# First tokens ahead of the conditioning weights in the load queue, and the opening of TensorE's list rewritten to the order of arrival

## The reference, cut to what matters

```python
shift, scale, gate = jnp.split(mod, 3, axis=-1)          # mod = silu(c) @ w_ada + b_ada
h = rmsnorm(x, rms_g) * (1 + scale) + shift
q, k, v, z_a, glu, z_b, gates = jnp.split(h @ w_in + b_in, PROJ_SPLITS, axis=-1)
```

## Time and profile before

| what | value |
|---|---|
| median of 3 runs | 1874.22 us (1873.65 to 1875.42) |
| the profiled execution, its own time | 1877.82 us |
| its span in the trace | 1875.6 us |
| TensorE busy in the span | 1829.8 us, 98% |
| chain of work that ended last, share of TensorE | 90% |

### The profile page before, as it was taken

How to read it: one execution, slowest core, us unless ns; L and a number is a source line. 1 busy time by engine, 2 the same in 40 slices (tenths; PEclk the granted TensorE clock), 3 DMA queues, 4 the chain that set the end, 5 groups by cost and what they waited for, 6 DMA issues and landing times.

```text
span 1875.6 us, 27263 instructions
## 1 busy us (share of the span) xinstructions
PE 1829.8 (98%) x10723; PEld 1561.1 (83%) x10723; DVE 1015.1 (54%) x1710; ACT 542.0 (29%) x1061; POOL 122.8 (7%) x205
## 2 busy tenths in 40 slices
PE   6999999999999999999999999999999899999998
PEld 3788899988888888888888888888888888888886
DVE  3544512111098338816870996766768555654444
ACT  3731101021111111211110114667768222322221
POOL 0100000000000000000000004322330000000000
PEclk9999999999999999999999999999999999999999
DMA  9524423143022112211220164997887767653321
GB/s 318 169 89 158 144 68 132 49 140 115 12 78 89 65 34 82 76 40 59 72 80 20 65 153 119 211 178 163 175 182 176 229 205 244 193 191 140 141 101 56
DMA packets 211145, 235.08 MB, mean 125 GB/s; under 512 B 47707, under 2 KB 157131, under 8 KB 207819
## 3 DMA queue, kind: packets, MB, share of 16 engines
q1 hardware_dynamic: 210760, 233.24, 42.5%
q10 hardware_dynamic: 259, 0.11, 0.0%
HBM read 152.52 MB, written 80.78 MB: 124 GB/s over the span
## 4 chain that ended last, share of the span: by engine, by line
PE 90%; SPq 4%; DMA 2%; issue 1%; ACT 1%; DVE 1%; POOLq 0%; DVEq 0%; POOL 0%; ACTq 0%
PE banks L789 17%; PE banks L790 17%; PE banks L791 17%; PE banks L1742 4%; PE banks L1741 4%; PE banks L1743 4%; PE banks L1713 3%; PE banks L1715 3%; PE banks L1714 3%; PE banks L1225 3%; SPq L1093 2%; PE banks L784 2%; PE banks L785 2%; PE banks L786 2%; PE banks L1191 2%
## 5 line engine op out<-in xcount | busy, mean ns | idle before, releaser
L789 PE MATMUL banks<-h_hi,w_hi 128*128 128x512 f32 (+1 forms) x1600 | 593.3, 371 | 3.6 <-DVE h_lo L598 2.5
L790 PE MATMUL banks<-h_lo,w_hi 128*128 128x512 f32 (+1 forms) x1600 | 589.4, 368 | 0.0
L791 PE MATMUL banks<-h_hi,w_lo 128*128 128x512 f32 (+1 forms) x1600 | 589.3, 368 | 0.0
L730 DVE SCALAR_TENSOR_TENSOR conv_acc<-glu_out,taps,conv_acc 128x773 f32<-128x773 f32 x360 | 371.5, 1032 | 12.3
L789 PEld LDWEIGHTS banks<-h_hi,w_hi 128*128 128x128 f32 x1600 | 301.8, 189 | 57.6 <-issue 3.4
L791 PEld LDWEIGHTS banks<-h_hi,w_lo 128*128 128x128 f32 x1600 | 301.8, 189 | 50.7
L790 PEld LDWEIGHTS banks<-h_lo,w_hi 128*128 128x128 f32 x1600 | 302.0, 189 | 49.0
L506 ACT ACTIVATE out_stage<-banks,param_cols 128x512 f32<-128x512 f32 (+1 forms) x120 | 77.0, 647 | 439.2 <-PE banks L791 433.2
L1713 PE MATMUL banks<-y_hi,wp_hi 128*128 128x512 f32 (+1 forms) x320 | 120.0, 375 | 4.9 <-DVE m_sum L1935 2.8
L1332 ACT ACTIVATE probs<-scores,stat 128x640 f32<-128x640 f32 (+2 forms) x128 | 106.7, 834 | 60.2 <-DVE stat L1259 58.6
L1715 PE MATMUL banks<-y_hi,wp_lo 128*128 128x512 f32 (+1 forms) x320 | 118.4, 370 | 0.0
(11 more groups left out here) (161 smaller groups left out, 2397.5 us busy)
## 6 DMA issues: line engine op xcount, KB each, us to landing
proj<-out_stage SPq DMA_DIRECT2D x96, 256.0 KB, 2.0
w_raw<-in_w_in SPq DMA_DIRECT2D x44, 512.0 KB, 3.9
gates_in<-proj SPq DMA_DIRECT2D x64, 256.0 KB, 2.9
k_hi<-k_hi_rows SPq DMA_DIRECT2D x16, 640.0 KB, 13.2
k_lo<-k_lo_rows SPq DMA_DIRECT2D x16, 640.0 KB, 15.2
w_ada<-in_w_ada SPq DMA_DIRECT2D x8, 1024.0 KB, 10.8
x_out<-in_x_sample SPq DMA_DIRECT2D x16, 512.0 KB, 3.4
out_y_sample<-x_out SPq DMA_DIRECT2D x15, 512.0 KB, 2.6
```

Source lines behind the costliest of these rows:

```text
L730: op = dve.scalar_tensor_tensor(dst, src, tap, dst, ALU.mult, ALU.add)
L789: pe.matmul(out, w_hi[:, s, k], h_hi[c][:, k], start=first, stop=False)
L790: pe.matmul(out, w_hi[:, s, k], h_lo[c][:, k], start=False, stop=False)
L791: op = pe.matmul(out, w_lo[:, s, k], h_hi[c][:, k], start=False, stop=last)
```

## The change

The change reorders the lists of the opening; no product is added or removed.

- SyncE: chunk 0's tokens are loaded first, in two halves with a semaphore each, and then the quarters of the conditioning weights, each followed by one column block. Before, quarter 0 came first, then the tokens.
- GpSimd: `RMS` has seven entries instead of six, since chunk 0 is done in halves.
- ScalarE and VectorE: the squares and the normalization of chunk 0 stand before the first row copy and the first coefficients; `modulate`, `split`, `high` and `low` stand in pairs behind the quarter that they need. On VectorE the two halves of chunk 1's normalization stand before and after `split(7)`.
- TensorE: `turn(0)` to `turn(2)` stand ahead of `ada_products(0)`; `ada_products(1)` stands ahead of the first `step`; the products of the three units are grouped by quarter, and `turn(8)` stands ahead of `step(6, [0, 1])`.
- The semaphore of the v bias serves chunk 0's first half as well, and is waited for at 32 where the bias is needed.

```diff
-RMS = [(0, 0, 4), (1, 0, 2), (1, 2, 2), (2, 0, 4), (4, 0, 2), (3, 0, 4)]
+RMS = [(0, 0, 2), (0, 2, 2), (1, 0, 2), (1, 2, 2), (2, 0, 4), (4, 0, 2), (3, 0, 4)]
...
-            if c == 1:
-                sp.dma_start(xs[c][:, 0:2], src[:, 0:2]).then_inc(x_half_in, 16)
+            if c < 2:
+                sp.dma_start(xs[c][:, 0:2], src[:, 0:2]).then_inc(x_half_in[c], 16)
                 sp.dma_start(xs[c][:, 2:4], src[:, 2:4]).then_inc(x_in[c], 16)
...
+        load_x(0)
         load_ada(0)
-        load_x(0)
+        load_w(sp, 0)
         load_ada(1)
-        load_w(sp, 0)
+        load_w(sp, 1)
         load_ada(2)
-        load_w(sp, 1)
+        load_w(sp, 2)
         load_ada(3)
-        load_w(sp, 2)
         load_x(1)
...
+        squares(0, 0)
+        squares(0, 1)
         row_of(0)
-        squares(0)
         high(0)
+        modulate(0)
+        modulate(1)
         row_of(1)
-        for s in range(4):
-            modulate(s)
         high(1)
+        modulate(2)
+        modulate(3)
+        high(2)
         row_of(2)
         modulate(4)
         modulate(5)
         row_of(3)
-        high(2)
         squares(1, 0)
...
+        normalize(0)
+        normalize(1)
         coefficients(0)
-        normalize(0)
         low(0)
+        split(0)
+        split(1)
+        low(1)
         coefficients(1)
-        for s in range(4):
-            split(s)
-        low(1)
+        split(2)
+        split(3)
+        low(2)
         coefficients(2)
         split(4)
         split(5)
-        low(2)
         coefficients(3)
         split(6)
+        normalize(2)
         split(7)
-        normalize(1)
-        normalize(2)
+        normalize(3)
...
-        ada_products(0)
         pe.wait_ge(rows_in, 16 * 7)
         pe.transpose(ps_rows, rows[0:R_C, :], cst.ident[0:R_C, 0:R_C]).then_inc(turned, 1)
         pe.transpose(ps_taps, taps[0:4 * TAPS, :], cst.ident[0:4 * TAPS, 0:4 * TAPS]).then_inc(turned, 1)
-        turn_row(0)
         pe.wait_ge(cols_out, 2)
-        ada_products(1)
         for s in range(3):
             turn(s)
+        ada_products(0)
+        turn_row(0)
+        ada_products(1)
+        step(0, [0])
+        step(1, [0])
         turn_row(1)
-        step(0, [0])
         turn(3)
-        step(1, [0])
         turn(4)
-        step(2, [0])
+        step(0, [1])
+        step(1, [1])
+        step(2, [0, 1])
         turn(5)
-        step(3, [0])
+        step(3, [0, 1])
+        turn(6)
         ada_products(2)
-        for s in range(4):
-            step(s, [1])
+        step(0, [2])
+        step(1, [2])
         turn_row(2)
+        step(2, [2])
+        step(3, [2])
         ada_products(3)
-        turn(6)
-        step(4, [0, 1])
+        turn(7)
+        step(4, [0, 1, 2])
         turn_row(3)
-        turn(7)
-        step(5, [0, 1])
-        for s in range(6):
-            step(s, [2])
+        step(5, [0, 1, 2])
+        turn(8)
         step(6, [0, 1])
-        turn(8)
+        turn(9)
         step(6, [2])
-        turn(9)
         step(7, [0, 1])
```

More of the change, by code:

```diff
@@ L248, in modulation @@
     ident_in, rows_in, c_in, x_in = sem("ident_in"), sem("rows_in"), sem("c_in"), [sem(f"x_in{c}") for c in range(5)]
-    x_half_in, wide_set = sem("x_half_in"), sem("wide_set")
+    wide_set = sem("wide_set")
     ada_in, gate_in, gb_in, vb_in = [sem(f"weights_in{i}") for i in range(8)], sem("gate_in"), [sem("gate_bias_in0"), sem("gate_bias_in1")], sem("vb_in")
+    x_half_in = [vb_in, sem("x_half_in")]
     tab_zero, tab_in, tab_out = sem("tab_zero"), sem("tab_in"), sem("tab_out")
@@ L447, in squares @@
         def squares(c, half=None):
-            act.wait_ge(x_half_in if half == 0 else x_in[c], 16)
+            act.wait_ge(x_half_in[c] if half == 0 else x_in[c], 16)
             for t in range(CHUNKS[c][1] // P) if half is None else range(2 * half, 2 * half + 2):
@@ L624, in front_dve @@
             if i == 10:
-                normalize(3)
+                normalize(4)
             if i == 16:
-                normalize(4)
+                normalize(5)
             if i == 19:
-                normalize(5)
+                normalize(6)
         pending = []
@@ L659, in front_dve @@
                 if n == 7 and c == 0:
-                    dve.wait_ge(vb_in, 16)
+                    dve.wait_ge(vb_in, 32)
                 s = slot_of[u]
```

## The result

| | before | changed |
|---|---|---|
| median, 7 runs each | 1875.01 us (1873.65 to 1877.53) | 1881.17 us (1877.51 to 1882.69) |
| the profiled execution, its own time | 1877.82 us | 1882.69 us |
| its span | 1875.6 us | 1880.5 us |

The ratio is 1.0029, with a 95% interval of 1.0019 to 1.0039: the kernel became slower by 5.4 us (3.6 to 7.3). The ratio is one of means; the two medians are 6.2 us apart. The forecast was slower, by 3.8 us. The changed kernel's median lies 0.7 us above the top of the range, 1880.5; against the median that the range was built on, 1874.22, the ratio gives 1879.7, inside it, near its top. The two profiled executions differ by 4.9 us, of which 3.4 arise before 65 us.

A forecast was written before the change was run, and what follows sets the result against it. TensorE, busy 1829.8 of 1875.6 us, was taken as the bound, so an opening shift reaches the end. Terms 0.3 + 1.4 + 2.1 = +3.8 us gave a median of 1878.0 us (1881.6 profiled), range 1874.3 to 1880.5.

The forecast's parts named there:

- The loads: SyncE's new order, no byte added: chunk 0 and quarter 0 by 17.2 us, quarter 1 at 25.0, quarter 3 at 40.7.
- The head: Start of TensorE's list: transpositions go before quarter 0; ready for quarter 1 between 23.9 and 26.7 us, taken as 25.1.
- From quarter 1 to quarter 3: TensorE's middle opening: quarter 1 at half clock ends at 28.8 us, quarter 3 ends at 44.9, before 44.65.
- From quarter 3 to turn(8): ScalarE and VectorE chain behind quarter 3: 10.46 us, turn(8) at 55.4 against 55.05, TensorE waiting five us.
- After turn(8): TensorE behind the pause: six more products on the path, 1.38 us, and a clock fall costing 2.1 us.
- The sum: Whole opening: later turn(8), six products and slow clock together make the kernel 3.8 us slower.
- a constant from there on: After the opening: both traces should differ by a constant, the opening's shift reaching the end unchanged.
- The clock did not hold: Rival at turn(8) or quarter 1: clock stays up or quarter 1 runs at full clock, 0 to +2.3 us; chance 0.14.
- The opening was not late: Rival at the head: chunk 0's second half last, transpositions at half clock, +1.2 to +1.6 us on top; chance 0.13.
- The change does what it says: Rival at turn(8): chunk 1 ready when TensorE is, by about 50.3 us, giving -3.6 us, 1870.7; chance 0.11.

The follow-up runs named there:

- e3: Changed kernel with chunk 1's squares moved ahead of row_of(3) and modulate(6) on ScalarE, its normalization ahead of coefficients(3) and split(7) on VectorE; ratio to the kernel before 0.9993.
- e1: Changed kernel with turn(8) back behind step(6, [0, 1]), as before the change; ratio to the kernel before 1.0013.
- e5: Kernel before with only turn(8) and turn(9) each moved ahead of the products they followed; ratio to the kernel before 1.0010.
- e2: Changed kernel with 18 unused products of 512 columns in the pause ahead of turn(8); ratio to the kernel before 0.9992.
- e6: The changed kernel as it is, measured again; ratio to the kernel before 1.0030.
- e11: Changed kernel with one unused product of 512 columns in the pause ahead of turn(8); ratio to the kernel before 1.0019.
- e4: e3 with all three units of step(6) ahead of turn(8) on TensorE; ratio to the kernel before 0.9991, and 0.9991 again when repeated.
- e7: Kernel before with 15 unused products of 512 columns ahead of turn(8); ratio to the kernel before 1.0003.
- e9: Kernel before with one unused product of 512 columns ahead of turn(8); ratio to the kernel before 0.9996.
- e10: Kernel before with 30 unused products of 512 columns ahead of turn(8); ratio to the kernel before 1.0010.
- e8: e4 with SyncE loading quarter 0 ahead of chunk 0's tokens, as in the kernel before; ratio to the kernel before 1.0013.

## Why the prediction was right

**The loads.** Chunk 0 was taken to arrive between 8.1 and 12.2: its squares started at 7.16 and 10.16, each as its half landed. Quarter 1 was put at 25.0; its products started at 24.68. Quarter 3 was no wait, as forecast. The second half of chunk 1 was put at 45.9 and landed at 46.1.

**The head.** TensorE was to be ready for quarter 1 between 23.9 and 26.7, and I took 25.1. The fold ended at 23.8 and it was weights that ended the pause. The transpositions took 2.79 us, close to the upper bound: TensorE had been idle for 3.42 us ahead of them and ran slowly.

**From quarter 1 to quarter 3.** Forecast 44.9, measured 44.60. Errors partly offset, and that the end fits to 0.3 us is in part luck. Quarter 1 started 0.4 us early and took 3.32 us and not 3.64, so that it ended at 27.9 instead of 28.8. It was not at half clock from its start: TensorE had come up to speed inside quarter 0, which took 3.38 us and not 3.64, and the granted clock fell to 0.50 only at 25.1, inside quarter 1. From there to quarter 3's end it took 16.7 us and not 16.1; 0.23 of that is a wait for `split(2)` at 33.17 that I had called covered, the rest I have not traced.

**From quarter 3 to turn(8).** Forecast 10.46 us, measured 55.23 - 44.60 = 10.63. The pause was put at five us and was 4.92. That it hangs on ScalarE's order behind quarter 3 and not on chunk 1's arrival is shown by e3, which moved `turn(8)` to 51.75 with every load in its place. That it does not depend on how early TensorE comes is shown by e1.

**After turn(8).** The six products were put at 1.38: e5 has 1.38 and e2 1.37. The clock was put at 2.1: e2 against the changed kernel has 1.86, and e1 has 1.6 after its shorter pause. That the clock would fall after five us was taken from a pause of 2.78; e1 adds 3.01 us (falls), e5 and e3 add 1.37 and 1.57 (stays). The estimate of 0.8 for this term, worked out from the price in the Trainium skill, "TensorE: Matmul & The Clock Gate", section "HAM oscillation", is too low here, and the measured stretch decides.

**The sum.** 0.3 + 1.4 + 2.1 = +3.8 was forecast for the opening; the marker has 0.18 + 1.37 + 1.86 = +3.41, and e6 repeats it with 3.51. With a scatter of about 0.6 us on the marker, that it comes within 0.4 of the forecast is in part luck; that the three terms add up exactly is arithmetic, since they are read from the same traces. The verdict is +5.4, and +5.6 in e6; e11, which differs by one unused product, has +3.6 (1.9 to 5.1). What was off is the step from the opening to the end: "a constant from there on" is what the traces show within their late scatter, up to five microseconds, but the timed runs put some 1.5 us more on the changed kernel on average, and less than the marker on the kernels with many fillers. Where that comes from stays open. What the opening does is read without it, and the direction stands: both intervals of the changed kernel, and that of e11, lie above 1.

**The rivals.** The clock did not hold. The opening was not late. "The change does what it says" was priced at -3.6 us under the condition that chunk 1 be ready when TensorE is. e4 meets that condition, by moving work that the change left in place: its markers are at -2.5 and -3.1.

## What to carry to other kernels

When a list is moved ahead on one engine, look for the first item in it that waits for another engine's chain, and ask what that chain hangs on. Here it hung on an event that the change did not move, so that the whole lead of TensorE turned into one pause, and the pause into a slow clock. Independent work (the squares of the next tokens) belongs in front of the instruction that waits for the late event, and everything that is ready belongs ahead of the item that waits. A few lines moved on ScalarE, VectorE and TensorE (e3, e4) turn +3.4 us of the opening into -2.5 to -3.1; in the timed runs, +5.4 us into about -1.7.

## What the runs showed of the hardware

- TensorE's granted clock fell with pauses of 3.01 and 4.92 us and stayed up after pauses of 1.37 and 1.57. It fell inside the pause of 4.92 us in the changed kernel (at 52.4) but only at about 55.6, after the pause, in e1. In the kernel before, and in all of e5, e7, e9 and e10, the pause of 1.51 us ahead of the first split h, which follows a fold, products of 2 columns each, was followed by a fall: the length of the pause alone does not decide. Products in the pause of e2 kept the clock up at no cost on the path.
- The row of the granted clock is no guide where the trace has not yet recorded a change. For the kernel before it reads, at 24 us,

```profile
24.00:25.00 1.00, 1.00 (x8) 1.00 1.10 341
```

  though quarter 1's products took 3.64 us there, twice the 1.85 of quarter 3. In e7 they also took 3.64 us, and its trace has a granted 0.50 at the same place. The durations are the surer reading.
- A product of 512 columns has a pitch of 0.43 us at the low clock and 0.23 at the high one.
- With the array busy ahead of it, quarter 1 took 1.92 us (e8); after a pause, between 2.53 (e2) and 3.64 (e4), though the pause of e2 was the longer, 2.10 us against 1.79. Up to there the two lists are the same, but the granted clock fell at 25.6 in e2, inside the products, and at 22.9 in e4, in the pause: the same list meets its clock change at another place in each execution.
- From the marker to the end of the span fourteen profiled executions took between 1810.6 and 1815.6 us. This late scatter of 5 us, against 1.2 us between the four executions that share the old opening, is the larger part of what makes the kernel hard to measure.
- Long runs of unused products cost less in the timed runs than in the trace (e7, e10), unexplained.
